# A two-block transformer kernel on one core: the modulation products move between the attention pairs, and ScalarE takes the heads out

## The reference, cut to what matters

```python
for l in range(DEPTH):                       # DEPTH = 2
    mod   = silu(c)     @ w_ada[l] + b_ada[l]
    mod_c = silu(c_ctx) @ w_ada[l] + b_ada[l]
    sh1, sc1, gt1, sh2, sc2, gt2 = split(mod, 6)          # and c* from mod_c
    h  = modulate(rms_norm(x, norm1_g[l]), sh1, sc1)      # hc from the context
    qa, ka, va, qb, kb, vb, ga, gb = split_in_proj(h @ w_in[l])
    ya = window_attention_latent(rope(qa), rope(ka), va, kac, vac, sink_a[l])
    yb = full_attention_latent(rope(rms_norm(qb)), rope(rms_norm(kb)), vb, kbc, vbc)
    x = x + gt1 * merge_branches(ya, yb, ga, gb, ...)
    x = x + gt2 * swiglu(modulate(rms_norm(x, norm2_g[l]), sh2, sc2), ...)
    # layer 0 only: the same for the context, with attention over context keys
```

## Time and profile before

| | us |
|---|---|
| median of 3 runs (lowest, highest) | 3656.03 (3651.72, 3657.26) |
| the profiled execution, and its span | 3653.35, 3651.6 |
| TensorE matmul busy | 3394.6 (93%) |
| VectorE, ScalarE, GpSimd busy | 1621.1, 1199.6, 375.9 |
| DMA moved 287.72 MB, mean | 79 GB/s |

### The profile page before, as it was taken

One profiled execution on the slowest core, in us unless ns is written; L12 is line 12 of the kernel. 1 busy time (PEld: TensorE's weight loads), 2 busy tenths in 40 slices (PEclk: granted clock), 3 DMA queues, 4 the chain that ended last, 5 costly groups with the idle time before them and its releaser, 6 DMA issues. The chain is left out here.

```text
span 3651.6 us, 51000 instructions
## 1 busy us (share of the span) xinstructions
PE 3394.6 (93%) x21104; PEld 2679.1 (73%) x21104; DVE 1621.1 (44%) x2708; ACT 1199.6 (33%) x1972; POOL 375.9 (10%) x285
## 2 busy tenths in 40 slices
PE   4999879899999989889899999889999998899998
PEld 3777658688888866667688777747888777478886
DVE  3233775422123244576422445574443355744432
ACT  2112664221113121365322333244222332442322
POOL 3110000200000021000630031210000002100000
PEclk9999999899999999999999999999999999999999
DMA  5331003211111235101222222002222320022222
GB/s 229 120 130 35 2 1 110 87 64 64 64 64 67 72 123 173 41 1 64 90 93 97 98 93 87 9 30 81 94 97 98 110 80 15 30 76 93 95 100 77
DMA packets 89693, 287.72 MB, mean 79 GB/s; under 512 B 8576, under 2 KB 25344, under 8 KB 88960
## 3 DMA queue, kind: packets, MB, share of 16 engines
q1 hardware_dynamic: 89472, 284.54, 22.9%
HBM read 282.40 MB, written 2.10 MB: 78 GB/s over the span
## 5 line engine op out<-in xcount | busy, mean ns | idle before, releaser
L454 DVE TENSOR_TENSOR w_low<-ring,w_high 128x1024 fp32r<-128x1024 f32 x418 | 528.5, 1264 | 1667.3 <-ACT w_high L451 1667.3
L509 PE MATMUL ps<-arena_r,w_high 128*128 128x512 f32 x3440 | 1067.7, 384 | 2.3 <-DVE arena L1815 1.2
L451 ACT ACTIVATE w_high<-ring 128x1024 fp32r<-128x1024 f32 x418 | 442.6, 1059 | 1625.4 <-PE ps L509 1617.4
L509 PE MATMUL ps<-high,w_high 128*128 128x512 f32 x2496 | 796.9, 367 | 63.9 <-DVE low L867 46.6
L509 PE MATMUL ps<-high,w_low 128*128 128x512 f32 x2496 | 790.2, 364 | 0.0
L509 PE MATMUL ps<-low,w_high 128*128 128x512 f32 (+1 forms) x2448 | 768.5, 362 | 0.0
L509 PEld LDWEIGHTS ps<-arena_r,w_high 128*128 128x128 f32 x3440 | 621.1, 188 | 154.6 <-issue 8.6
L509 PEld LDWEIGHTS ps<-high,w_high 128*128 128x128 f32 x2496 | 421.3, 190 | 173.2 <-issue 75.3
L509 PE MATMUL ps<-arena_r,w_low 128*128 128x512 f32 (+1 forms) x1328 | 498.0, 389 | 0.0
L509 PEld LDWEIGHTS ps<-high,w_low 128*128 128x128 f32 x2496 | 421.5, 190 | 79.1
L509 PEld LDWEIGHTS ps<-low,w_high 128*128 128x128 f32 x2448 | 413.2, 190 | 79.1 <-issue 0.4
(11 more groups left out here) (335 smaller groups left out, 2767.8 us busy)
## 6 DMA issues: line engine op xcount, KB each, us to landing
ring<-in_weights SPq DMA_DIRECT2D x428, 512.0 KB, 3.4
arena<-in_ada SPq DMA_DIRECT2D x80, 512.0 KB, 5.2
high_f<-in_ada SPq DMA_DIRECT2D x16, 512.0 KB, 5.2
xL<-in_x SPq DMA_DIRECT2D x1, 2048.0 KB, 9.9
out<-xL SPq DMA_DIRECT2D x1, 2048.0 KB, 6.3
low_f<-in_low_rank SPq DMA_DIRECT2D x3, 512.0 KB, 4.4
const<-in_const SPq DMA_DIRECT2D x1, 1168.0 KB, 5.4
xC<-in_ctx SPq DMA_DIRECT2D x1, 1024.0 KB, 12.0
```

The lines of the kernel that those rows point to most:

```text
L451: act.activation(w_high[:, slot, :], ring[:, place, :], ACT.Copy).then_inc(unit_high.sem, 1)
L454: dve.tensor_tensor(w_low[:, slot, :], ring[:, place, :], w_high[:, slot, :].bitcast(F32), ALU.subtract).then_inc(unit_free.sem, 1)
L509: mm = pe.matmul(bank(4 * (c % 2) + 2 * p + s, width), w, g.split[k][s][x], start=(n == 0 and m == 0), stop=(n == len(part) - 1 and m == 2))
```

## The change

`ModulationBeside` is a new form of `Modulation` which hooks into `attention`. Layer 0's attention carries two of them: the 32 units `rest` of layer 0, one in each of iterations 1 to 32, and then the 16 units of layer 1 in iterations 36 to 47. Layer 1's attention carries its own 32, in iterations 1 to 28 (four iterations have two). They are issued between the transposes of pair i-1 and the values of pair i-2. Units now come as two transfers of 256 KB into four places, from SyncE's queue in the attention block, which before held nothing there. The output of the values moves by 384 columns and shares bank 7 with the modulation sums. As a matmul with `start` would act on the whole bank, values no longer start but add onto zeros: ScalarE writes them (`clear`, a copy of the identity scaled by 0) after each heads(i-2), and each unit and each values wait for that.

For every attention, those of the second block too: ScalarE, not VectorE, copies the heads out; the copies of the transposed probabilities go back into `probs`, which has three turns, and the array `turned` goes; both exponentials come first and both sink exponentials after them, with a semaphore of their own, so scores(i) no longer wait for a sink. The input projections and the output projection of the first block keep no modulation part.

```diff
+        class ModulationBeside(Modulation):
+            def sync_parts(self, sync):
+                if self.sets:
+                    sync.wait_ge(scores_in.sem, scores_in.at(64))
+                for n in range(self.units):
+                    if self.earlier + n >= len(self.halves):
+                        sync.wait_ge(ada_used.sem, ada_used.at(max(self.earlier, self.earlier + n - len(self.halves) + 1)))
+                    src = dram["ada"][(self.l * 6 * D // ADA_COLS + self.block0) * 2 + n]
+                    for m, half in enumerate(self.halves[n % len(self.halves)]):
+                        sync.dma_start(half, src[:, m * 512:m * 512 + 512]).then_inc(self.landed(n).sem, 16)
+            def tensor_parts(self, pe, i):
+                for n in range(self.units):
+                    if self.when[n] == i:
...
+                        for j in range(4):
+                            mm = pe.matmul(ps[32 * j:32 * j + 32, self.BANK_AT:self.BANK_AT + ADA_COLS],
+                                           cond[:, 4 * (n % 2) + j, 30 - 2 * b:62 - 2 * b],
...
+                        mm.then_inc(ada_used.sem, 1)
+                if i == self.last + 2:
+                    pe.wait_ge(rows_out.sem, rows_out.at(self.sets + 1))
...
+            def scalar_parts(self, act, i):
+                if i == self.last + 1:
...
+                    act.activation(rows[:, :], ps[:, self.BANK_AT:self.BANK_AT + ADA_COLS], ACT.Copy).then_inc(rows_out.sem, 1)
+                elif i == self.last + 2:
+                    act.wait_ge(groups_in.sem, groups_in.at(self.sets + 1))
+                    act.activation(rows[:, 0:64], ps[:, self.BANK_AT + ADA_COLS:self.BANK_AT + ADA_COLS + 64],
+                                   ACT.Copy).then_inc(groups_out.sem, 1)
+            def vector_parts(self, dve, i):
+                if i == self.last + 3:
+                    dve.wait_ge(groups_out.sem, groups_out.at(self.sets + 1))
+                    self.finish_columns(dve, rows[:, 0:64], self.sets + 1)
...
-            return Stage(gemms, ToZ(), normed, inner=[Heads(l), Modulation(l, 8, 16, when, places)])
+            return Stage(gemms, ToZ(), normed, inner=[Heads(l)])
...
-            T_AT, O_AT = 2048, 3584
+            T_AT, O_AT = 2048, 3584 + 384
...
                         if 0 <= i - 1 < n:
                             turn(i - 1)
+                        for part in beside:
+                            if part.busy(i):
+                                pe.wait_ge(heads_out.sem, heads_out.at(max(i - 2, 0) + 1))
+                            part.tensor_parts(pe, i)
                         if 0 <= i - 2 < n:
                             values(i - 2)
...
                     for i in range(n + 3):
-                        if 0 <= i - 3 < n:
-                            heads(i - 3)
                         if 0 <= i - 1 < n:
                             normalize(i - 1)
                         if i < n:
                             maxima(i)
+                        for part in beside:
+                            part.vector_parts(dve, i)
...
                     def exponent(i, e):
...
-                        if i >= 2:
-                            act.wait_ge(turned_in.sem, turned_in.at(2 * (i - 2) + e + 1))
+                        if i >= 3:
+                            act.wait_ge(heads_in.sem, heads_in.at(i - 2))
...
+                    def heads(j):
+                        act.wait_ge(heads_in.sem, heads_in.at(j + 1))
+                        return act.activation(pairs[j]["y"], ps[:, O_AT:O_AT + P], ACT.Copy)
+                    def clear():
+                        return act.activation(ps[:, O_AT:O_AT + P], con("ident"), ACT.Copy, scale=0.0)
...
+                    for i in range(n + 2):
                         if i < n:
                             exponent(i, 0)
                             exponent(i, 1)
+                            if pairs[i]["sink"] is not None:
+                                sink(i)
+                        if 0 <= i - 1 < n:
                             copy(i - 1, 0)
                             copy(i - 1, 1)
+                        if i >= 2:
+                            ins = heads(i - 2)
+                            for part in beside:
+                                part.scalar_parts(act, i)
+                            if beside:
+                                chain_s.link(act, ins)
+                                ins = clear()
+                            ins.then_inc(heads_out.sem, 1)
...
-            attention(pairs1(l), HD ** -0.5)
+            if both:
+                rest = ModulationBeside(l, 8, 16, [1 + n for n in range(32)], places)
+                queries = [(z[:, Z_QA + n, 0:S], z[:, Z_QA + n + 1, 0:S]) for n in range(0, 8, 2)]
+                ahead = ModulationBeside(1, 0, 8, [36 + n * 12 // 16 for n in range(16)], queries, rest)
+                attention(pairs1(l), HD ** -0.5, [rest, ahead])
+            else:
+                attention(pairs1(l), HD ** -0.5, [ModulationBeside(l, 8, 16, [1 + n * 28 // 32 for n in range(32)], places)])
...
-            chain1 = [Stage([merge], sums, split_here=True), Stage([out], Residual(16), inner=ahead)]
+            chain1 = [Stage([merge], sums, split_here=True), Stage([out], Residual(16))]
```

More of the change, by code:

```diff
@@ L686, in vector_parts, with finish_columns @@
                     dve.wait_ge(groups_in.sem, groups_in.at(1))
[L687 to L701, removed]
+                    self.finish_columns(dve, ps[:, self.BANK_AT + ADA_COLS:self.BANK_AT + ADA_COLS + 64], 1)
+            def finish_columns(self, dve, groups, sets):
+                c0, n = 2 * self.block0, 2 * self.blocks
+                for s in range(2):
+                    for h in range(2):
+                        got = groups[:, 32 * h:32 * h + n].rearrange("p (b s) -> p b s", s=2)[:, :, s]
+                        out = mod[:, c0:c0 + n, s].rearrange("p (b h) -> p b h", h=2)[:, :, h]
+                        bias = col(f"b_ada{self.l}", c0, n).rearrange("p (b h) -> p b h", h=2)[:, :, h]
+                        ins = dve.tensor_tensor(out, got, bias, ALU.add)
+                ins.then_inc(mod_out.sem, 1)
+                dve.wait_ge(mod_out.sem, mod_out.at(sets))
+                g = 0 if self.block0 == 0 else 1
+                first = 24 * g + KD
+                for s in range(2):
+                    dve.scalar_tensor_tensor(gain[:, g, :, s], mod[:, first:first + KD, s], 1.0,
+                                             col(f"{('g1', 'g2')[g]}{self.l}", 0, KD), ALU.add, ALU.mult)
             def finish(self):
@@ L1324, in clear_of, with sinks @@
                 return max(0, i - 1)
+            def sinks(i):
+                return sum(pair["sink"] is not None for pair in pairs[:i])
             def turned_at(i, e):
@@ L1751, in build @@
             out.z0 = 0
-            ahead = [Modulation(1, 0, 8, [n * 4 // 16 for n in range(16)],
-                                [high_f[:, n * UNIT:(n + 1) * UNIT] for n in range(5)])] if both else []
-            chain1 = [Stage([merge], sums, split_here=True), Stage([out], Residual(16), inner=ahead)]
+            chain1 = [Stage([merge], sums, split_here=True), Stage([out], Residual(16))]
             normed = Norm(both, lambda k, s: gain[:, 1, k, s:s + 1], lambda k, s: mod[:, 24 + k, s:s + 1])
```

93 lines of the change are left out of this document (60 added, 33 removed).

## The result

| | before | after |
|---|---|---|
| median, us | 3654.64 (4 runs) | 3604.35 (4 runs) |
| lowest, highest | 3651.72, 3657.26 | 3601.48, 3607.43 |
| span of the profiled execution | 3651.6 | 3599.7 |

The ratio is 0.9866 with a 95% interval of 0.9854 to 0.9878.

A forecast was written before the change was run, and what follows sets the result against it. TensorE was taken to bound the dense stages and a loop of waits the attentions. 42.4 us saved less about 10 of costs gave net 32.4, so 3621 on the profiled execution and 3624 us as median, range 3609 to 3645.

The forecast's parts named there:

- What bounds the stages: Dense stages bound by TensorE; attentions by a loop of scores, two maxima, two exponentials, with transposes and values in its shadow.
- What goes away: Modulation units leaving both input projections and the output projection: 16.6, 17.1, 7.5 and 1.2 for regroupings, 42.4 us saved.
- Gain of the rewriting: Latent pairs: scores released without waiting for a sink, 0.17 or 0.1 a pair, about 2 us a layer less 0.6.
- It just fits: Full pair's iteration: with a unit TensorE is free at 428.03, release due at 428.12; a unit costs 0 to 0.15 us.
- the tails: Ends of the attentions, where last values wait for regrouping or for head and clear: +2.0 us layer 0, +0.9 layer 1.
- The other costs: Attentions beyond single latent units: double iterations 1.8, slow clock 1.5, context pairs 1.0 and 1.2, tails; all costs about 10 us.
- The slow stretch of the clock: Near the start of layer 1's attention, 13.5 us at clock 0.50: 1.5 us of the early units stays visible.
- TensorE as bound: Attentions: waits and drains make a unit 0.9 to 1.1 us, costing 25 to 42; 3638 to 3656 us, chance 0.15.
- The clear as gate: Attentions: units and values wait for ScalarE's clear; gain gone at 1.6 us for head and clear, 3674 at 1.8; chance 0.06.
- No shrinking: Dense stages stay as long because something else would be due: 3666 us, chance 0.03.
- Free ride: Attentions: units cost 0.44 or less, or extra work keeps the clock full: 3616 to 3608 us, chance 0.10.
- The range: Whole kernel: 3609 to 3645 us, taking in the free ride's upper half and the lower half of TensorE as bound.

The follow-up runs named there:

- e1: The kernel before without the 80 modulation units of the input and output projections, constants in their place: 3600.20 us against 3651.57, ratio 0.9864.
- e4: The kernel before with the same units gathered in fewer groups, threes and fours, in the two input projections: 3641.14 us against 3651.57, ratio 0.9971.
- e9: The changed kernel with every attention unit after a set's first cut to one small matmul, waits and loads kept: 3598.29 us, ratio 0.9849 to the kernel before.
- e2: The changed kernel with no modulation in the attentions, constants in its place: 3594.60 us, ratio 0.9844 to the kernel before.
- e6: The changed kernel with the units of both attentions starting in iteration 5, not 1: 3605.66 us, 1.4 more than the changed kernel run again.

## Why the prediction was wrong, point by point

- **What bounds the stages: right.** The dense stages were TensorE's alone: without the units they are 51.7 us (e1) and 52.3 us (after) shorter in sum. The attention's loop is scores, maxima, exponentials, scores, with room for a unit: the latent pairs of layer 0 take 155.9 us, as before.
- **What goes away: the first step that failed, a term that was mis-sized.** It was put as "from the start of a unit's matmuls to the next L509", 42.4 us; it measured 51.4 (e1) to 52.3 (after). The interval leaves out what is lost before the first matmul of a group and in the first ones behind it; e4 gives 0.33 a group, and 0.13 of it was counted. Both sides of it could be had from the trace of before: 0.44 and 0.46 beside a unit where the stream has 0.35.
- **Gain of the rewriting: a little too small.** "About 2 us a layer, less 0.6" for the clears: the steps gave 2.6 a layer (0.19 and 0.14, where 0.17 and 0.1 were forecast), and the clears cost nothing, as e9's steps are e2's.
- **"It just fits": right in the mean, wrong in the place.** I had TensorE tight in full pairs' iterations and free in windowed ones. It is the other way round: 0.40 and 0.57 free in the first, and the unit shows in two of the windowed ones. The sum for the full iteration counted the 0.17 ahead of the values once by itself and once within the 0.57; and the windowed one was read at the pair whose values have 512 keys, not at w3, where they have 640. Both errors are small, and units cost 5.3 by matmuls (e9) and 2.6 by the tails, 7.9, where the forecast had some 13 before the gain.
- **The other costs.** A double iteration costs 0.43 as priced, but only in windowed ones, so two of layer 1's four (5.12 and 5.44 in place of 4.70 and 5.00). Sinks at the context pairs cost 0.20 each, not 0.13; doubled units there cost 0.37 in two of four iterations. The context pairs came out 2.0 us longer where 2.2 was forecast, the tails 1.7 and 0.9 where 2.0 and 0.9.
- **The slow stretch of the clock: the second step that failed.** It was put at a cost of 1.5 us in layer 1 and at nothing in layer 0. The first three steps, in which it lies, are 1.8 us shorter in layer 0 and 2.2 in layer 1, 0.3 of each by the rewriting. With the steady latent steps (-0.4 and +0.2, where +0.8 and +2.6 were forecast) that is the attentions' +0.4 for +10. The shorter stretch is luck as far as the forecast goes: no run shows what sets it.
- **The rivals.** TensorE as bound: partly, for eight steps a layer, with 0.09 or 0.39 each. The clear as gate: no. No shrinking: no. Free ride: its 3616 to 3608 was the nearest, but its reasons (a cheaper unit, the clock raised by the units) were not what happened: the unit costs 0.57, and e2 to e6 speak against the units as the cause of the shorter slow stretch.
- **The range** was built from doubts about the attention and held none about the dense stages, whose price looked read off the rows. That is where one half of the 20 us were; the other half was in the attentions.

## What to carry to other kernels

Price a foreign group of matmuls in a full TensorE stage by comparing whole tiles with and without it, not by its own rows: it costs on both sides, here 0.33 us a group beside 0.44 us of work a unit. If such groups have to stay in a dense stage, gather them (e4: 8.3 us by stage for the same work in 25 fewer groups). Work moved into a loop of waits is cheap (7.9 us here for 52), but the room differs from iteration to iteration; double it once on the chip, and the steps show roughly where to put it.

## What the runs showed of the hardware

- In the attention a unit of 128 x 32 tiles had 0.17 us of idle weight loads ahead of it (427.73) and 0.41 behind it (428.30), the latter with most of its own matmuls. In the dense stages a group of units cost 0.33 us beside 0.44 a unit (e4): 0.09 ahead, 0.11 behind, 0.13 within.
- Behind two 128 x 128 matmuls of the rotation, in the same array shape, the first two of the stream took 0.75 us from start to start in after, not 0.35.
- ScalarE wrote 128 x 128 float32 into PSUM in 0.28 us (L1527, median of 82), and read as many out of PSUM in 0.28 to 0.29 (L1524).
- The granted clock fell to 0.50 at the start of both large attentions in every trace, for 3.4 to 13.7 us. In layer 1 two executions of one kernel had the same length, and kernels with the same attention had others (before 13.7, e1 6.8, e4 3.4); in layer 0 two executions of the changed kernel had 3.4 and 6.8.
